# One step of a threshold search moved ahead of the relu or residual of its unit, with one step in each of 31 units

## The reference, cut to what matters

```python
score = jnp.einsum('bqh,bqhs->bqs', wib, jax.nn.relu(logits))
score = jnp.where(causal[None], score, -jnp.inf)
_, idx = lax.top_k(score, topk)            # topk = 256
...
def channel_mixer(x, g_norm, w1, w2):
    h = rms_norm(x, g_norm)
    return x + jnp.square(jax.nn.relu(h @ w1)) @ w2
```

## Time and profile before

| What | Value |
|---|---|
| Median of the runs | 2132.42 us |
| Profiled execution: time | 2130.93 us |
| Profiled execution: span | 2129.2 us |
| TensorE busy | 2088.3 us, 98% of the span |
| VectorE busy | 1335.6 us, 63% |
| ScalarE busy | 993.0 us, 47% |
| GpSimd busy | 1019.4 us, 48% |
| Mean granted clock of TensorE | 0.998 of full speed |

### The profile page before, as it was taken

How to read it: one execution, slowest core, us unless ns; L and a number is a source line. 1 busy time by engine, 2 the same in 40 slices (tenths; PEclk the granted TensorE clock), 3 DMA queues, 4 the chain that set the end, 5 groups by cost and what they waited for, 6 DMA issues and landing times.

```text
span 2129.2 us, 29538 instructions
## 1 busy us (share of the span) xinstructions
PE 2088.3 (98%) x9850; PEld 1742.6 (82%) x9850; DVE 1335.6 (63%) x2197; ACT 993.0 (47%) x1498; POOL 1019.4 (48%) x634
## 2 busy tenths in 40 slices
PE   7999899999999999999999999999999999999999
PEld 6888677888878898888888888888878888888887
DVE  7697657545481345268777645879853321779877
ACT  6554565665623564333323245435354323464552
POOL 6865753654646003556556556859774655000000
PEclk9999999999999999999999999999999999999999
DMA  5321112333323012223333232334323423433433
GB/s 215 99 64 57 70 38 62 109 99 99 99 70 109 21 53 80 89 80 111 97 99 100 89 92 90 106 89 139 99 89 99 135 93 113 144 119 109 139 128 119
DMA packets 69313, 208.30 MB, mean 98 GB/s; under 512 B 6976, under 2 KB 7232, under 8 KB 68928
## 3 DMA queue, kind: packets, MB, share of 16 engines
q1 hardware_dynamic: 69040, 206.57, 30.4%
q10 hardware_dynamic: 144, 0.02, 0.0%
HBM read 200.28 MB, written 6.29 MB: 97 GB/s over the span
## 4 chain that ended last, share of the span: by engine, by line
PE 87%; DVE 4%; issue 2%; ACT 1%; POOL 1%; DMA 0%; DVEq 0%; ACTq 0%; POOLq 0%; SPq 0%
PE psum L879 22%; PE psum L881 22%; PE psum L880 22%; PE psum L1225 5%; PE psum L1223 5%; PE psum L1224 5%; PE psum L1056 3%; PE psum L903 2%; PE psum L1032 1%; PE psum L1033 1%; POOL w_buf L1249 1%; PE psum L961 1%; PE psum L971 0%; PE psum L886 0%; DVE psum L2239 0%
## 5 line engine op out<-in xcount | busy, mean ns | idle before, releaser
L1249 POOL TENSOR_TENSOR w_buf<-raw,w_buf 128x1024 fp32r<-128x1024 f32 x270 | 659.4, 2444 | 488.4 <-ACT w_buf L1579 477.5
L879 PE MATMUL psum<-hid_buf,w_buf 128*128 128x512 f32 x1088 | 425.8, 391 | 0.0
L881 PE MATMUL psum<-hid_buf,w_buf 128*128 128x512 f32 x1088 | 423.7, 389 | 0.0
L880 PE MATMUL psum<-hid_buf,w_buf 128*128 128x512 f32 x1088 | 423.6, 389 | 0.0
L1579 ACT ACTIVATE w_buf<-raw 128x1024 fp32r<-128x1024 f32 x256 | 269.6, 1054 | 269.2 <-PE psum L881 216.0
L879 PE MATMUL psum<-h_buf,w_buf 128*128 128x512 f32 x960 | 376.7, 392 | 5.8 <-DVE xt L2411 4.1
L881 PE MATMUL psum<-h_buf,w_buf 128*128 128x512 f32 x960 | 373.7, 389 | 0.0
L880 PE MATMUL psum<-h_buf,w_buf 128*128 128x512 f32 x960 | 373.6, 389 | 0.0
L2434 DVE SCALAR_TENSOR_TENSOR psum<-y_buf,wdw,psum 128x512 f32<-128x512 f32 x435 | 294.9, 748 | 0.0
L880 PEld LDWEIGHTS psum<-hid_buf,w_buf 128*128 128x128 f32 x1088 | 204.4, 188 | 42.8 <-issue 0.7
L881 PEld LDWEIGHTS psum<-hid_buf,w_buf 128*128 128x128 f32 x1088 | 204.2, 188 | 42.9
(11 more groups left out here) (350 smaller groups left out, 3194.9 us busy)
## 6 DMA issues: line engine op xcount, KB each, us to landing
raw<-weights SPq DMA_DIRECT2D x320, 512.0 KB, 3.5
w_more<-weights SPq DMA_DIRECT2D x36, 512.0 KB, 3.9
xt<-x_t SPq DMA_DIRECT2D x2, 2048.0 KB, 8.2
out_t<-xt SPq DMA_DIRECT2D x16, 256.0 KB, 2.0
x_in<-x_t SPq DMA_DIRECT2D x12, 256.0 KB, 6.9
early<-weights SPq DMA_DIRECT2D x4, 512.0 KB, 7.6
x_kept<-xt SPq DMA_DIRECT2D x1, 2048.0 KB, 9.0
h_first<-x_kept SPq DMA_DIRECT2D x1, 2048.0 KB, 7.9
```

The lines of the kernel that those rows point to most:

```text
L879: nc.tensor.matmul(acc, lhs_hi, rhs_hi, start=first, stop=False)
L880: nc.tensor.matmul(acc, lhs_hi, rhs_lo, start=False, stop=False)
L881: return nc.tensor.matmul(acc, lhs_lo, rhs_hi, start=False, stop=last)
L1249: nc.gpsimd.tensor_tensor(dst_lo, src, dst_hi.bitcast(F32), ALU.subtract).then_inc(done, 1)
```

## The change

The two tables get other values, and VectorE's `key_unit` is called ahead of the relu or the residual of its unit instead of behind it. Before, the steps lie in three of four units (2, 3, 4, 6, 7, 8, ... 42) and the selections in units 43, 44, 45, 46, which are down units. After, each of the units 1 to 31 holds one step, and the selections lie in 33, 35, 37, 39, which are up units. ScalarE's code is unchanged apart from the table that it reads: a Sign stays behind `hidden_hi` of its unit.

```diff
-KEY_AT = [0] + [int(at % 4 > 0) for at in range(42)] + [0] * 5
-KEYS_DONE_AT = {43: 0, 44: 1, 45: 2, 46: 3}
+KEY_AT = [0] + [1] * KEY_BITS + [0] * 16
+KEYS_DONE_AT = {33: 0, 35: 1, 37: 2, 39: 3}
...
                         for r in range(16):
+                            key_unit(16 * q + r)
                             if r < 8:
                                 relu_scaled(r // 4, r % 4)
                             else:
                                 add_residual(down, half)((r - 8) // 4, r % 4)
-                            key_unit(16 * q + r)
```

## The result

The changed kernel takes 2180.64 us (median of five runs, 2180.06 to 2182.53) against 2132.42. The ratio is 1.0229, with a 95% interval of 1.0216 to 1.0241: 48 us slower. The forecast was 2174.3, in a range of 2160 to 2182.

The account below looks back on a forecast made before the run. TensorE, busy 98% of the span, was taken as the bound, so only its standing still counts: 22.0 + 13.3 + 7.6 - 5.2 + 4.2 = +41.9 us on 2132.4 gives 2174.3, range 2160 to 2182.

Parts of the forecast that it names:

- The new loop: Up units with a step: relu, Sign, step, relu run in turn, 7.46 us against TensorE's 5.44, 2.02 lag per relu.
- Who waits for a late relu: First down unit: TensorE waits for the eighth hidden tile, with 0.9 us of slack; PSUM banks and weights give none there.
- Rival (b): Units 16 to 23: three units of slack swallow the lag, only the start hurts; 16.8 us slower, 2149; chance 0.06.
- Rival (d): Up units: loop shorter than TensorE's unit, Sign done when VectorE asks; faster, 2127, or 2131; chance 0.06.
- Units 0 to 8 and 16 to 24: Layer-0 MLP, first half: late relus cost TensorE +22.0 us in units 0 to 8 and +13.3 in units 16 to 24.
- A slow restart: Units 8 and 24: TensorE runs slowly after long waits, 2.1 us once per group; +4.2 us, ends 0 and 8.4.
- Units 32 to 40: Selections in up units make relu 39 late, plus half of possible GpSimd waits: +7.6 us, ends 4.6 and 10.6.
- What is removed: Units 43 to 52: all that the selections cost there before goes away, -5.2 us.
- rival (c): More slow time at short waits or restarts, and every selection meets GpSimd's passes: +49.1 us, 2181.5 and above; chance 0.06.

Follow-up runs that it names:

- the order alone: The changed kernel with the tables of before (selections in units 43 to 46), each step still ahead of its relu or residual: 2150.4 us, ratio 1.0089.
- Cutting the loop on ScalarE's side: The changed kernel, but ScalarE does the Signs of a step ahead of the square of the same unit's relu: 2143.8 us, ratio 1.0055.
- the fillers: The changed kernel with 22 unread matmuls ahead of each wait for the seventh and eighth hidden tile in units 8 and 24: 2176.5 us, ratio 1.0201.

## Why the prediction was right

**The new loop** was right in mechanism and size: 7.46 us worked out from four rows, 7.48 in the trace, 7.46 and 7.47 in the order alone. Relu 7 was put at 413.9 and came at 413.89; unit 4 at 372.5 and came at 372.07. The agreement to 0.01 us is luck: the stretch had begun 0.38 us earlier, and the last round took 7.75 (406.14 to 413.89). Cutting the loop on ScalarE's side took all 16.0 us of units 9 to 25 away and 21.0 of the 25.0 of units 0 to 9.

**Who waits for a late relu** was right: the hidden tiles of the first down unit, seventh and eighth, and no PSUM bank. That weights would stop nobody was right for unit 24 and not for units 7 and 8, which waited 1.28 and 1.69 us for theirs; it adds nothing to the sum, because the seventh and the eighth tile come when the loop lets them. Rival (b), the slack of three units, falls by the 5.8 us wait at 521.04. Rival (d), no loop, falls by the 3.63 us that VectorE waited for ScalarE before a step.

**Units 0 to 8 and 16 to 24** were forecast at 22.0 and 13.3. (The starts given for the 22.0, 418.4 and 396.61, are 21.8 apart.) With the restarts taken off, 2.7 and 2.2, they measured 22.3 and 13.8.

**A slow restart** was due, but mis-sized: 2.1 a group measured 2.7 and 2.2 (the rate was the expected one, but it lasted 5.65 and 4.69 us and not 4.3), and I left the third group out, where it cost 1.5. The term of 4.2 was 6.4. The half rate at the very start had a granted clock of 1.00 beside it; here the column does show it.

**Units 32 to 40** is the term most off: 7.6 forecast, 12.7 measured, above its upper end of 10.6 even with the 1.5 of restart taken off (11.2). One wait of 2.0 us per selection was assumed and half of it taken. The runs showed three waits in each of the last three selections (lines 2239, 2244 and 2248), 4.5 us in all in the third (3.13 - 2.02, 1.53 - 0.22, 3.13 - 1.09, against the same lines where GpSimd is idle), while line 2238, whose 2.63 us had been the model, did not wait (0.75 in the third). Each selection there stands between the relus that feed GpSimd: two hidden tiles and two splits, 7.4 us of GpSimd's work, fall into every 12 us or so. The trace of before could have warned of it: beside the 2.63, its line 2244 took 1.53 in the first selection and its line 2248 1.82 in the second, each beside a split. Against that, closing computation and first selection together took 12.25 us instead of 16.0, since GpSimd was idle then (line 2218, 2.32 us before, took 0.16).

**What is removed**, 5.2, measured 5.4.

The terms' errors add up to the 6.3 us between 41.9 and 48.2, and the result lies 1.4 us under the upper end of the range. In its time it lies at rival (c), 2181.5: three of the four selections meet GpSimd, more than (c) took for it, and restarts cost more than I took, if less than (c)'s 8.4; units 5 to 8 did not run slower at their short waits, which (c) allowed for as well (19 matmuls in the 4 us from 378, and again from 392). Unit 4 did restart at half rate (0.80 us for its first matmul, 0.59 of the clock from 372 to 376), which the loop hid: units 7 and 8 waited for splits anyway.

## What to carry to other kernels

When work is moved ahead of an instruction in one engine's list, follow every semaphore that it waits for back to its own list, and see whether it comes from behind that same instruction one round earlier: if so, two engines that ran side by side now take turns. Add up the loop from rows and compare it with the time per unit; slack of several units hides a lag only until someone needs the last of the late results. Filling idle time of VectorE is worth nothing in itself: the version that won kept the steps behind the relu or residual, had them done earlier, and set the long pieces two units apart, where three units of slack absorb them.

## What was not expected of the hardware

- A TensorTensorScan that reads one SBUF tile twice and writes PSUM also waits beside GpSimd (line 2239: 2.02 us alone on 896 columns, 3.13 beside GpSimd), and GpSimd's own pass beside it lasts 4.12 us instead of 2.40: by their ends the waits go both ways.
- Even an instruction on 128 x 1 elements waits until GpSimd's pass ends (line 2244: 0.22 us alone, 1.53 beside it).
- The granted clock was already below 1.00 after waits of 3.0 (0.62), 3.7 and 4.3 us, and at 1.00 after waits of 1.7 and 2.4 us and of 2.8 (unit 4 where the Signs go first): waits that look small cost up to three quarters as much again (2.8 us after the wait of 3.70). The length of the wait does not give the price: after 4.34 and 4.33 us at unit 4, eight matmuls lost 1.6 us in the changed kernel and 14 lost 3.0 in the order alone, and after 5.42 us at unit 40 seven lost 1.5 and, with the fillers, 13 lost 2.7. Why they differ stays open.
- 88 useless matmuls made the kernel 4.1 us faster, by keeping the granted clock at 1.00 over waits of 6.7 and 5.8 us.
